# Expert weights loaded with 8 KB of consecutive bytes per partition, in a mixture-of-experts trunk on one Trainium2 core

## The reference

```python
def hier_moe(x2d, w_group, b_group, w_expert, b_expert, w1, w3, w2):
    ...   # each token picks one group of four experts, and two experts in it
    def expert_step(acc, p):
        w1e, w3e, w2e, c = p
        h = jax.nn.silu(x2d @ w1e) * (x2d @ w3e)
        return acc + c[:, None] * (h @ w2e), None
```

## Time and profile before

| what | value |
|---|---|
| median of 3 runs | 841.06 us (834.59 to 842.97) |
| profiled execution | 839.87 us |
| its span, first to last instruction | 837.8 us |
| TensorE busy | 708.5 us, 85% |
| VectorE, ScalarE busy | 310.4 us and 217.7 us |
| chain that ended last | PE 53%, DMA 19%, DVE 18% |
| DMA queue of SP (q1) | 176.24 MB in 80880 packets |

### The profile page before, as it was taken

How to read it: one execution, slowest core, us unless ns; L and a number is a source line. 1 busy time by engine, 2 the same in 40 slices (tenths; PEclk the granted TensorE clock), 3 DMA queues, 4 the chain that set the end, 5 groups by cost and what they waited for, 6 DMA issues and landing times.

```text
span 837.8 us, 17693 instructions
## 1 busy us (share of the span) xinstructions
PE 708.5 (85%) x6878; PEld 455.0 (54%) x6879; DVE 310.4 (37%) x932; ACT 217.7 (26%) x528; POOL 20.2 (2%) x38
## 2 busy tenths in 40 slices
PE   5999979988989989865669999969973899998874
PEld 4887858644555645433248557747841455554431
DVE  0599961361222212210155106861262122221215
ACT  1312651241212212110340014563140122222230
POOL 0000000000000000000200001100000000000001
PEclk9999989989999999987679999999987899999996
DMA  9997042403793999999399925030627964927904
GB/s 304 367 392 268 1 138 82 170 0 135 290 395 141 372 397 354 352 357 339 126 326 387 388 93 213 9 143 0 215 86 270 396 263 175 406 76 275 349 27 151
DMA packets 94858, 193.30 MB, mean 231 GB/s; under 512 B 8144, under 2 KB 22329, under 8 KB 94825
## 3 DMA queue, kind: packets, MB, share of 16 engines
q1 hardware_dynamic: 80880, 176.24, 57.4%
q10 hardware_dynamic: 11673, 8.10, 3.2%
q0 software_dynamic: 2272, 8.52, 2.8%
HBM read 181.84 MB, written 11.01 MB: 230 GB/s over the span
## 4 chain that ended last, share of the span: by engine, by line
PE 53%; DMA 19%; DVE 18%; issue 5%; ACT 4%; SPq 1%; DVEq 0%; ACTq 0%; POOLq 0%
DMA ring<-in_moe_w 16%; PE ps L638 14%; DVE work L1095 9%; PE ps L659 7%; PE ps L565 4%; PE ps L537 3%; PE ps L548 3%; PE ps L718 3%; PE ps L737 3%; PE ps L610 2%; PE ps L476 2%; PE ps L510 2%; PE ps L621 2%; DMA ring<-in_conv_w_pw 1%; DMA work<-ybuf,pos_i 1%
## 5 line engine op out<-in xcount | busy, mean ns | idle before, releaser
L638 PE MATMUL ps<-ring,work 128*32 128x256 f32 x2816 | 173.5, 400 | 45.7 <-issue 30.8
L638 PEld LDWEIGHTS ps<-ring,work 128*32 128x32 f32 x2816 | 101.6, 115 | 110.1 <-issue 64.3
L827 ACT ACTIVATE work<-ps 128x256 f32<-128x256 f32 (+3 forms) x154 | 52.2, 354 | 223.2 <-PE ps L659 95.7
L1290 DVE TENSOR_TENSOR work<-work,ps 64x256 f32<-64x256 f32 x44 | 18.7, 424 | 236.2 <-ACT work L913 236.2
L659 PE MATMUL ps<-ring,work 128*32 128x256 f32 x1408 | 89.8, 383 | 0.6 <-DMA ring<-in_moe_w 0.6
L1095 DVE SCALAR_TENSOR_TENSOR work<-work,wdw 128x272 f32<-128x272 f32 x180 | 74.9, 499 | 0.0
L610 PE MATMUL ps<-tok,work 128*32 128x256 f32 x928 | 64.7, 386 | 0.0
L476 PE MATMUL ps<-xT,ring 128*128 128x272 f32 x256 | 61.0, 401 | 2.9 <-DMA ring<-in_conv_w_pw 2.3
L659 PEld LDWEIGHTS ps<-ring,work 128*32 128x32 f32 x1408 | 38.9, 109 | 33.6 <-DVE work L1292 10.3
L476 PEld LDWEIGHTS ps<-xT,ring 128*128 128x128 f32 x256 | 49.5, 195 | 13.7 <-issue 2.4
L913 ACT ACTIVATE work<-ps 64x256 f32<-64x256 f32 x44 | 16.6, 376 | 148.2 <-PE ps L638 148.2
(11 more groups left out here) (215 smaller groups left out, 725.5 us busy)
## 6 DMA issues: line engine op xcount, KB each, us to landing
ring<-in_moe_w SPq DMA_DIRECT2D x138, 1024.0 KB, 11.5
ring<-in_conv_w_pw SPq DMA_DIRECT2D x12, 1024.0 KB, 11.9
ybuf<-work ACTq DMA_DIRECT2D x44, 128.0 KB
ybuf<-const POOLq DMA_DIRECT2D x2, 2048.0 KB, 8.5
ring<-in_kv_w_k SPq DMA_DIRECT2D x4, 1024.0 KB, 8.9
ring<-in_kv_w_v SPq DMA_DIRECT2D x4, 1024.0 KB, 10.8
ring<-in_attn_w_q SPq DMA_DIRECT2D x4, 1024.0 KB, 10.8
ring<-in_attn_w_o SPq DMA_DIRECT2D x4, 1024.0 KB, 12.4
```

Of the source, the lines that this page charges most:

```text
L638: last = pe.matmul(ps[SLOTS * q:SLOTS * (q + 1), 0, 0:256], xTg[:, k, :], w[:, k, (q % 2) * 256:(q % 2 + 1) * 256], start=(k == 0), stop=( ...
L827: return act.activation(dst, src, ACT.Copy)
```

## The change

Channels are dealt to partitions differently. For w1 and w3 row r goes to partition r // 8 (`(p k)`): a partition's 8 rows are 16 KB in one run, and a half brick takes 8 KB of it. w2's rows go in pairs, 2p and 2p + 1 of each 256, to partition p: also 8 KB in one run. The number of loads, their bytes, their order and the waits before them are unchanged, four halves in flight.

What multiplies these weights has to follow. `tok` is kept with its channels reordered: ScalarE's moves out of PSUM write them in steps of 128 floats (`tok_columns`), eight to a group; the gather and the transposes behind it are then unchanged. The transposes of `hs` (L646) take every second column. Where `tok` is added to rows in their normal order (L521, L1311), it is read in steps of 128 floats. The one addition on VectorE that was 1024 wide (the third token tile, 16 rows) becomes two of 512. Nothing else moves on any engine.

```diff
+        def tok_columns(rows, j, half):
+            return tok[0:rows, j, :].rearrange("t (k x) -> t x k", k=NC_)[:, 64 * half:64 * half + 64, :]
+        def by_eight(t):
+            return t.rearrange("t (x k) -> t x k", k=NC_)
...
-                    load_half(b + m, half, NC_ if m < 2 else 4, src.rearrange("(k p) n -> p k n", p=P))
+                    if m < 2:
+                        load_half(b + m, half, NC_, src.rearrange("(p k) n -> p k n", p=P))
+                    else:
+                        sp.dma_start(brick(b + m).rearrange("p (a m n) -> p a m n", a=2, m=2)[:, half],
+                                     src.rearrange("(a p m) n -> p a m n", a=2, m=2)[:, half]).then_inc(sem(f"brick{(b + m) % RING}_{half}"), 16)
...
-                    pe.matmul(ps[:, 6 + j, :], ident, tok[:, j, half], start=True, stop=False)
+                    pe.matmul(ps[:, 6 + j, :], ident, tok_columns(P, j, 1), start=True, stop=False)
...
-                    last = pe.transpose(ps[:, 4, m * 64:(m + 1) * 64], hs[64:128, m * P:(m + 1) * P], ident[64:128, 64:128])
+                    last = pe.transpose(ps[:, 4, m * 64:(m + 1) * 64], hs[64:128, m:256:2], ident[64:128, 64:128])
...
-                        move(tok[0:rows_, j, half * 512:(half + 1) * 512], ps[0:rows_, 2 * j + half, :]).then_inc(sem(f"tok_ready{l}"), 1)
+                        move(tok_columns(rows_, j, half), by_eight(ps[0:rows_, 2 * j + half, :])).then_inc(sem(f"tok_ready{l}"), 1)
...
-                    step(dve.scalar_tensor_tensor(first, first, wts[0:n, 0, j:j + 1], tok[0:n, j, 0:w], ALU.mult, ALU.add))
+                    for h in range(w // 512):
+                        part = by_eight(first[:, h * 512:(h + 1) * 512])
+                        step(dve.scalar_tensor_tensor(part, part, wts[0:n, 0, j:j + 1], tok_columns(n, j, h), ALU.mult, ALU.add))
```

## The result

The changed kernel takes 845.59 us (median of 7 runs, 841.89 to 850.53), the kernel before 839.41 beside it: ratio 1.0071, 95% interval 1.0037 to 1.0106. It is slower by some 6 us, where 3 us faster was forecast. The profiled execution took 841.89 us, its span is 839.8 (before: 839.87 and 837.8).

What follows compares the result with a forecast made beforehand. Loads were taken to bind only layer 0's second half, TensorE's items layer 1. Terms -8.4 + 4 + 0.8 + 0.6 = -3.0 us took the profiled 839.87 us to 836.9, stated as 837.5; range 825 to 850.

Steps and rivals of the forecast that it cites:

- The loads: Layer 0's second half: 8 KB packets take 0.24 us off each of 40 half bricks, -9.6 us, bounds 7.2 and 12.
- What comes back in layer 0: Layer 0: slow stores cost only where TensorE waits for loads anyway; 1.2 us of the gain comes back, leaving -8.4.
- The stores in layer 1: Layer 1: stores alternate with 8 KB packets one for one, land after 15.5 us, hold ScalarE: +4 us, bounds 0 and 12.
- the store that was named: Layer 1's third group of loads: store from 712.4 lands at 732.5; move of y before 726.48 waits 6.5 us.
- in more than one stretch: Layer 1: the forecast called itself wrong if the stores set the time in more than one stretch.
- The stepped transposes: TensorE's weight loads of L646, every second float near to contiguous: taken as 0, bounds 0 to +12 us if doubled.
- The tokens' steps: Accesses to `tok` in steps of 128 floats, on ScalarE's moves, L521 and L1311: +0.8 us; twice as slow +3.6.
- The fetches: Two TensorE jumps ahead of layer 1 wait for instruction fetches behind larger load packets: +0.6 us, bounds 0 and +14.
- Rival 1: Stores aren't held back, as queues share otherwise beyond 4 KB: 827 to 832, say 829 us; chance 0.25.
- Rival 2: Queue waiting goes by packets, not time: jumps ahead of layer 1 14 us later, stores land after 22; 863 us; chance 0.17.
- Rival 3: 8 KB runs are cut into 4 KB packets, 836 us, or reads 16 KB apart are slower, 842; chance 0.08.

Runs made afterwards that it cites:

- experiments 7: The kernel before with four staging buffers for the items' results instead of two, and no other change: 835.5 us, ratio 0.9955.
- 5: The changed kernel with four staging buffers and the step of two floats moved from TensorE's transposes to ScalarE and VectorE: 828.0 us, ratio 0.9842.
- experiments 9: The changed kernel with its two staging buffers, only the step of two floats moved from TensorE's transposes to ScalarE and VectorE: 842.8 us, ratio 1.0084.
- the first experiment: The changed kernel with four staging buffers for the items' results instead of two, nothing else changed: 832.7 us, ratio 0.9934.
- experiment 11: The kernel of experiment 5 with layer 0's stores alone issued as four DMAs over all 16 engines: 825.0 us, ratio 0.9848.
- experiment 10: The kernel of experiment 5 with layer 1's tokens written and read in adjacent floats (output is another function): 826.2 us, ratio 0.9858.
- 12: The kernel before, without 8 KB runs, with four staging buffers and layer 0's stores as four DMAs over 16 engines: 828.1 us, ratio 0.9894.
- 8: The changed kernel with two staging buffers, each item's store issued as four DMAs over 16 engines: 837.0 us, ratio 0.9962.

## Why the prediction was wrong

- **The loads** were right. 2.88 us a half were forecast, 2.84 measured; -9.6 us in layer 0 were forecast, and with the stands and the step gone it is 200.5 to 190.5, -10.0 (experiments 7 and 5). With them it was only -3.6.
- **What comes back in layer 0** is the step that failed: "In layer 0 the same hold falls where TensorE would wait for loads anyway; the 1.2 us above stand for it." The forecast had nothing left to pay for them there beyond the 1.2 us; the runs show 6.8 us (experiments 9 and 5: 197.3 and 190.5). Beside the first experiment the changed kernel loses only 2.9, since that one's jumps ran 3.2 us longer at the low clock. Four of the waits end at 299 to 330 us, in items in which TensorE didn't wait for the ring before; its waits were all in the last three items. Some does come back there, as forecast: up to the last two items experiment 9 is 10.4 us behind the fifth, and these two then take 24.4 us instead of 28.0. But it is a third and not all, because what is used later is loaded again later: the chain of loads, which began at 273 us before, begins at 344, behind some 8 us in which the DMA engines are busy 0.2 or less (the view is at experiment 11).
- **The stores in layer 1** had the right mechanism, place and wait: one for one at 320 ns (353 forecast), a landing 18.2 us behind the start of the issue (15.5 forecast), ScalarE's wait of 6.90 us before the store that was named (6.5), and 3.87 at TensorE (4.2). The term was +4, measured +7.9 for the layer. It lacks the lower clock behind the stand, 2.8 us, which I had seen in the earlier trace rows and not priced here, and 1.4 us for the step (20 x 0.07). The second store in layer 1's chain, 14.55 us, costs nothing: the item is 9.58 us long with two buffers and with four. So the sign "in more than one stretch" didn't come.
- **The stepped transposes**, taken as 0 within a bound of 12: 202 for 137 ns, 0.1 us an item, some 3 to 4 us in 44 items with four buffers, and nothing measurable beside the stands (experiment 9). "Every second float is near to contiguous" was wrong. So is the page's rule for this read (the Trainium skill, Advanced Engine Details and Errata, "Memory Cachelines"): two hits on each line, and yet 47% longer. For PSUM reads of ScalarE and VectorE with the same step the time is unchanged.
- **The tokens' steps**, +0.8 forecast: the instructions are longer (VectorE's first addition of 128x512 takes 1.08 us for 0.74), but experiment 10 sees some 0.3 us of it in layer 1's trace and none in the kernel's time. For layer 0 it stays open.
- **The fetches**, +0.6: 11.19 us for 11.22, nothing in this pair. But a pair can't tell: the same wait was 8.88 and 6.04 us in experiments 7 and 12, which load as before, and in those with 8 KB runs throughout (1, 5, 8, 9, 10, 11) 8.12 once and 12.0 to 12.3 else. So 8 KB runs may cost some us there; no experiment separates it.
- **Rival 1** (stores not held back) is out by the 320 ns. The rule that would lead to it (the Trainium skill, DMA: Bandwidth & Descriptors, "Queues, rings and completion order"), whole drains of 9 to 17 descriptors, doesn't agree with the 5 to 10 store packets in each half microsecond either. **Rival 2** (the queue's wait goes by packets) is out by the jumps: it wanted 14 us more ahead of layer 1, and no kernel has over 12.31 there where 11.22 stood before. Landings of over 17 us came all the same, from stores queued behind one another. **Rival 3** is out by the 39664 packets and, for slower reads, by the 2.84 us a half.
- **Two readings** were a little off and change nothing: the items of layer 1 were taken as 7.0 us, by the silus they are 7.12 and 7.21 in turn; and a 4 KB packet of the earlier trace rows takes 0.274 x 16 x 2.4 us / 69 = 152 ns, not 155 to 160.

The trace's own sum: 200.5 to 196.9 in layer 0, 149.7 to 157.6 in layer 1, +0.8 between, is +5.1, near the medians' +6.2 (its execution was the fastest of the seven). Ahead of layer 0's first silu the profiled execution of after is 3.0 us quicker than that of before, which makes the spans look closer. The kernels of the experiments begin their first silu between 195.5 and 200.1 us, with and without the change in no order, so I don't count it as an effect.

What stays open: why the clock falls behind some gaps of 2.6 us and not behind others, and what sets the wait ahead of layer 1. The forecast range, 825 to 850, holds the measured time, but only because it is wide; the sign was wrong.

## What to carry to other kernels

Larger packets sped up the stream here and slowed down the small stores that share its engines, packet for packet. Before enlarging the one, work out how long the other then takes to land and how many buffers its producer needs (here two more buffers turned +0.7% into -0.7%, though 0.45% of that they bring without larger packets too). With the stores on four engines the whole ring was slower (2.84 us a half for 2.56), so spread small stores over all engines where the issuing engine has the time. Price a stall with the slower clock behind it, and a stride by moving it to another engine. And ask where the hidden wait falls: one in an early item isn't paid back in full by a limit that binds the last ones.

## What the runs showed of the hardware

- A 1 KB store packet gets one turn per ring packet: on each engine one per 120, 200 and 320 ns beside packets of 2, 4 and 8 KB.
- A gap of 2.59 us on TensorE cost 1.8 us more or nothing, by whether the clock fell behind it; a gap of 3.87 us cost 2.8 more.
- A step of two floats in SBUF lengthens TensorE's weight loads of 64x128 from 137 to 202 ns and the matmuls from 233 to 291; the same step in PSUM leaves ScalarE's silu at 375 ns and VectorE's product at 424.
- ScalarE's four issues took 1.76 us, one 0.55.
- TensorE's wait ahead of layer 1, for nothing that the profile shows, was 6.04, 8.88 and 11.22 us in three kernels that load alike (experiments 12 and 7, the kernel before).
